# mLSTM heads' inverse root: one power operation on GpSimd in place of ScalarE's square root and VectorE's reciprocal

## What is computed

```python
h = num / jnp.maximum(jnp.abs(den), jnp.exp(-m_t))[..., None]
...
hm = mlstm_chunkwise(mq, mk, mv, log_i, log_f)
hm = rms_norm_2(hm, out_norm_g.reshape(M_HEADS, M_V_DIM)).reshape(B, L, M_WIDTH).astype(x.dtype)
ym = hm * jax.nn.sigmoid(mo) * jax.nn.silu(mgate)
...
y = jnp.concatenate([ya, ym], axis=-1) @ w_out.astype(x.dtype)
```

## Time and profile before

| | us |
|---|---|
| median of 3 runs | 1455.07 (1453.48 to 1455.53) |
| the profiled execution itself | 1452.7 |
| its span | 1450.9 |
| TensorE busy | 1431.7 (99%) |
| VectorE busy | 1092.5 (75%) |
| ScalarE busy | 853.9 (59%) |
| GpSimd busy | 273.1 (19%) |
| share of TensorE, VectorE, ScalarE in the chain that ended last | 88%, 7%, 3% |

### The profile page before, as it was taken

How to read it: one execution, slowest core, us unless ns; L and a number is a source line. 1 busy time by engine, 2 the same in 40 slices (tenths; PEclk the granted TensorE clock), 3 DMA queues, 4 the chain that set the end, 5 groups by cost and what they waited for, 6 DMA issues and landing times.

```text
span 1450.9 us, 27343 instructions
## 1 busy us (share of the span) xinstructions
PE 1431.7 (99%) x9657; PEld 1320.6 (91%) x9657; DVE 1092.5 (75%) x2021; ACT 853.9 (59%) x1559; POOL 273.1 (19%) x329
## 2 busy tenths in 40 slices
PE   8999999999999999999999999999999999999988
PEld 7888899988888888889988888999999999999988
DVE  6777679877766777667787766888778769876883
ACT  6665458766645656445566654556756555576752
POOL 1111113121111111024031112422240125121000
PEclk9999999999999999999999999999999999999999
DMA  6667754556655666555456656544344555434443
GB/s 212 200 189 211 239 178 132 182 178 200 191 188 181 193 190 187 186 192 174 147 177 199 197 165 181 169 132 115 98 128 136 168 146 147 140 90 136 133 129 119
DMA packets 247875, 241.25 MB, mean 166 GB/s; under 512 B 15456, under 2 KB 246736, under 8 KB 247784
## 3 DMA queue, kind: packets, MB, share of 16 engines
q1 hardware_dynamic: 244888, 236.73, 53.5%
q10 hardware_dynamic: 2896, 3.30, 0.8%
HBM read 238.92 MB, written 1.07 MB: 165 GB/s over the span
## 4 chain that ended last, share of the span: by engine, by line
PE 88%; DVE 7%; ACT 3%; issue 2%; DMA 1%; ACTq 0%; DVEq 0%
PE bank L652 79%; DVE w_lo L1818 2%; ACT w_hi L1084 1%; DVE work L2410 1%; PE bank L951 1%; PE bank L969 1%; PE bank L934 1%; PE bank L880 1%; DVE work L1851 1%; PE bank L890 1%; DVE work L2433 1%; ACT L1112 1%; PE bank L950 1%; DMA work<-in_x_dram 1%; PE bank L970 0%
## 5 line engine op out<-in xcount | busy, mean ns | idle before, releaser
L652 PE MATMUL bank<-x_both,w_hi 128*128 128x512 f32 (+2 forms) x3552 | 805.0, 332 | 0.5 <-DVE h L1914 0.5
L1818 DVE TENSOR_TENSOR w_lo<-raw,w_hi 128x1024 fp32r<-128x1024 f32 (+1 forms) x456 | 552.6, 1235 | 214.9 <-ACT w_hi L1084 213.9
L1084 ACT CAST w_hi<-raw 128x1024 fp32r<-128x1024 f32 (+1 forms) x456 | 457.1, 1029 | 135.7 <-PE bank L652 117.9
L652 PEld LDWEIGHTS bank<-x_both,w_hi 128*128 128x128 f32 x3552 | 515.1, 189 | 3.7 <-DVE w_lo L1818 0.6
L652 PE MATMUL bank<-x_both,w_lo 128*128 128x256 f32 (+1 forms) x2480 | 496.7, 281 | 0.0
L652 PEld LDWEIGHTS bank<-x_both,w_lo 128*128 128x128 f32 x2480 | 432.1, 189 | 62.6
L652 PE MATMUL bank<-y_both,w_hi 128*128 128x512 f32 (+2 forms) x1472 | 346.9, 338 | 5.7 <-DVE w_lo L1818 3.6
L652 PEld LDWEIGHTS bank<-y_both,w_lo 128*128 128x128 f32 x1088 | 191.7, 188 | 31.3
L652 PEld LDWEIGHTS bank<-y_both,w_hi 128*128 128x128 f32 x1472 | 213.3, 189 | 7.1 <-DVE w_lo L1818 4.5
L652 PE MATMUL bank<-y_both,w_lo 128*128 128x256 f32 (+1 forms) x1088 | 215.8, 280 | 0.0
L1705 POOL TENSOR_TENSOR work<-work,rstd 128x256 f32<-128x256 f32 x88 | 66.9, 781 | 412.3 <-ACT work L1149 412.3
(11 more groups left out here) (306 smaller groups left out, 1231.1 us busy)
## 6 DMA issues: line engine op xcount, KB each, us to landing
raw<-in_ffn_w_in_dram SPq DMA_DIRECT2D x176, 512.0 KB, 4.0
raw<-in_w_in_dram SPq DMA_DIRECT2D x100, 512.0 KB, 3.7
raw<-in_ffn_w_out_dram SPq DMA_DIRECT2D x64, 512.0 KB, 4.5
raw<-in_w_out_dram SPq DMA_DIRECT2D x32, 512.0 KB, 3.6
raw<-in_ffn_w_out_dram SPq DMA_DIRECT2D x32, 384.0 KB, 3.6
raw<-in_rec_w_in_dram SPq DMA_DIRECT2D x16, 512.0 KB, 4.2
raw<-in_sg_w_in_dram SPq DMA_DIRECT2D x16, 512.0 KB, 4.2
raw<-in_rec_w_out_dram SPq DMA_DIRECT2D x8, 512.0 KB, 3.5
```

What stands on the lines that cost most here:

```text
L652: i_ = mm(accs[m][:, cols], w[:, s, j, m * P:(m + 1) * P], moving, start=begin and g == 0 and not residual, stop=final)
L1084: nc.scalar.copy(w_hi[:, s, 0:n, :], raw[:, s, 0:n, :]).then_inc(hi_made, 1)
L1818: TT(w_lo[:, s, 0:n, :], raw[:, s, 0:n, :], w_hi[:, s, 0:n, :].bitcast(fp32), SUB).then_inc(lo_made, 1)
```

## The change

The inverse root becomes one operation on GpSimd, s_b = d_max ^ (-1/2), with the exponent from a one-column tile broadcast along the row. The factor 1/16 that ScalarE applied moves into the sum: TensorE's L1018 takes a broadcast column of 1/16 in place of ones, and VectorE's L2398 multiplies by 16 EPS in place of 256 EPS. ScalarE loses, per head, both table loads, both dummies and the root; VectorE loses the reciprocal. `taken` stays where it was and waits for GpSimd's `m_sb`. In `taken`'s place for heads 0 to 2 nothing else moves. ScalarE's square into d_max now waits for the previous head's power, since GpSimd reads that tile.

```diff
@@ TensorE, step 2
-                            i_ = mm(bank[5][:, 0:L], ones[:, :], n_sq[:, w, :], start=w == 0, stop=w == 1)
+                            i_ = mm(bank[5][:, 0:L], sixteenth[:, 0:1].broadcast_to((P, P)), n_sq[:, w, :], start=w == 0,
+                                    stop=w == 1)
@@ ScalarE, step 1, step 2 and head_root
                         i_.then_inc(m_sq, 1)
+                        if n:
+                            act.wait_ge(m_sb, n)
                         activation(d_max, bank[4][:, 0:L], ACT.Square).then_inc(m_dsq, 1)
                     if stage == 2:
-
-                        root_table()
                         roots_due.append(n)
...
-                        act.wait_ge(ms_read, n + 1)
                         if n % M_H < M_H - 1:
                             act.wait_ge(m_den, n + 1)
                             floor_to_all(l, n % M_H + 1)
-                        if n:
-                            act.wait_ge(m_sb, n)
-                        activation(d_root, d_max, ACT.Sqrt, scale=1.0 / 16).then_inc(m_root, 1)
-                        exp_table()
@@ GpSimd, start
             nc.gpsimd.memset(eps_sq[:, :], EPS * EPS)
+            nc.gpsimd.memset(sixteenth[:, :], 1.0 / 16)
+            nc.gpsimd.memset(minus_half[:, :], -0.5)
             nc.gpsimd.memset(epsc[:, :], EPS).then_inc(ones_set, 1)
@@ GpSimd, end of each layer
                     pool.wait_ge(h_final, NC8)
+                for n in range(M_H * l, M_H * (l + 1)):
+                    pool.wait_ge(ms_read, n + 1)
+                    if n:
+                        pool.wait_ge(m_taken, n)
+                    TT(s_b, d_max, minus_half[:, 0:1].broadcast_to((P, L)), POW).then_inc(m_sb, 1)
+                if l == 0:
                     h_squares(7, "proj0", 0)
@@ VectorE, step 2, inverse_root, taken
-                        STT(out=d_max, in0=d_max, scalar=256 * EPS, in1=bank[5][:, 0:L], op0=MUL, op1=ADD).then_inc(ms_read, 1)
+                        STT(out=d_max, in0=d_max, scalar=16 * EPS, in1=bank[5][:, 0:L], op0=MUL, op1=ADD).then_inc(ms_read, 1)
...
-                def inverse_root(n):
-
-                    dve.wait_ge(m_root, n + 1)
-                    V.reciprocal(s_b, d_root).then_inc(m_sb, 1)
-
                 def taken(hd, stage):
                     n = M_H * l + hd
                     if stage == 3:
-                        if hd == M_H - 1:
-                            inverse_root(n)
                         dve.wait_ge(m_sb, n + 1)
...
                                 if n[0]:
-                                    inverse_root(M_H * l + n[0] - 1)
                                     taken(n[0] - 1, 3)
```

More of the change, by code:

```diff
@@ L230, in build_stack @@
     ALU, ACT = mybir.AluOpType, mybir.ActivationFunctionType
-    MUL, ADD, SUB, MAX, MIN = ALU.mult, ALU.add, ALU.subtract, ALU.max, ALU.min
+    MUL, ADD, SUB, MAX, MIN, POW = ALU.mult, ALU.add, ALU.subtract, ALU.max, ALU.min, ALU.pow
     dram = dict(ffn1_w_in=ffn1_w_in, ffn1_w_out=ffn1_w_out, ffn2_w_in=ffn2_w_in, ffn2_w_out=ffn2_w_out,
@@ L270, in build_stack @@
         x_sums = sb("x_sums", [P, 2])
+        sixteenth = sb("sixteenth", [P, 1])
+        minus_half = sb("minus_half", [P, 1])
         work = sb("work", [P, WORK_SLOTS * L])
```

## The result

| | before | after |
|---|---|---|
| median of 4 runs each, same chip | 1454.28 us (1453.37 to 1455.53) | 1766.49 us (1765.70 to 1768.44) |
| ratio, 95% interval | | 1.2151 (1.2136 to 1.2166) |
| span of the profiled execution | 1450.9 us | 1763.9 us |

The kernel became 312.2 us slower, where 7.2 us of gain were forecast and the range ended at 1487. The page of the changed kernel first: busy times, granted clock, shares of the chain that ended last, and the groups of the power and of `taken` (busy, mean ns | idle before and its releaser). The edit moved the lines: L2398 of before is L2404, L2372 is L2378, L2386 is L2392, L2421 is L2420, L2433 is L2432, L1009 is L1011, L1018 is L1020, L652 is L654, L1818 is L1824; L2441 is L2440, L2446 is L2445, L2456 is L2455; the power is L1801.

What follows compares the result with a forecast made beforehand. VectorE's loop, slower than TensorE's by 0.85 and 1.34 us a head, was taken to bound the head stretches. TensorE's 7.7 us of idle less 0.5 gave -7.2 us, from 1455.07 to 1447.9 us; range 1446 to 1451, 8 in 10 to 1487.

Steps and rivals of the forecast that it cites:

- The price of the power: GpSimd's power over 128x272, once per head: 2.8 us, as 4.3 times a product's 0.64 us.
- The forecast's upper end: Far end taken for GpSimd's power: twenty product passes, 12.8 us, giving a kernel time of about 1520 us.
- the slow rival: VectorE stands at `taken` between heads, TensorE behind it; 6 us per us of power beyond 3.7; chance 0.40.
- the prediction's free formula: Without contention: six times r's excess over 3.87 us between heads, twice `taken`'s lateness against 9.31 us behind last heads.
- r = power + 0.2: Time from the sum step's end (L2398) to `taken`: the power plus two handovers of 0.1 us, 3.0 us.
- The forecast's own case: A power of 2.8 us closes nearly all TensorE waits in the heads' stretches: -7.2 us, 1447.9 us.
- the 7.7 us of idle: TensorE's idle in the two mLSTM head stretches, claimed as all the change can give back.
- the 0.5 us off for contention: Taken off the gain for what may be left of layer 1's 3.3 us of projection waits.
- The cover of the squares: Squares queued on GpSimd behind the fourth power, released 21 us after L2398; a longer power would bare them.
- Contention: Behind last heads, GpSimd's power may lock out VectorE's two-input steps throughout, `taken` coming 4.5 + power after L2398; even chance.

Runs made afterwards that it cites:

- 40 columns: The changed kernel with the power over 40 of the 272 columns, the other 232 left out: 1468.37 us, ratio 1.0099.
- the run with the product: The changed kernel with the power turned into a GpSimd product of the same shape, the inverse root left out: 1442.76 us, ratio 0.9924.
- 17 columns: The changed kernel with the power over 17 of the 272 columns, the other 255 left out: 1442.61 us, ratio 0.9925.
- the run of shapes: The kernel before with five extra GpSimd powers of different shapes on their own tiles, nobody waiting for them: 1453.45 us, ratio 1.0005.

## Why the prediction was wrong

- **The step that failed is "The price of the power".** It took 4.3 times a product, 2.8 us, from the ratio of VectorE's reciprocal to VectorE's maximum. The measured price is 43.75 us, 68 products and 16 times the step's value. The forecast's upper end, twenty products or 12.8 us, was chosen and not read from a row; the truth lies 3.4 times beyond it, and so the range of the time failed too. The neighbouring row came from another engine, on which the reciprocal is one instruction of 1.85 us; GpSimd's rows had only sums, products and memsets and said nothing of a function. The prediction said that itself ("nothing in the trace bounds a function made of many steps") and then bounded it.
- **The mechanism was right**, that of the slow rival: VectorE standing at `taken`, w_lo and the next scores queued behind it, TensorE waiting for these. With the measured 43.8 us the prediction's free formula gives 6 x (43.81 - 3.87) = 239.6 between heads and 2 x (43.94 - 9.31) = 69.3 behind the last, 308.9 us together; measured 312.2. For 40 columns it gives +13.3 against +14.7. What it left out is the slower clock after the stalls, which can explain a rest of this size (3.6 us behind the last heads).
- **The small terms.** The prediction took r = power + 0.2; it is power + 0.11. The sum step's new constant and the broadcast column of L1020 cost nothing that was seen, as costed; the run with the product has both and is fast.
- **The forecast's own case** (a power near 2.8 us) was run with 17 columns: it gains 11.1 us, where 7.2 were forecast for it. Here the 7.7 us of idle, by the prediction "all that a change here can give back", was too small: TensorE's weight loads waited 10.2 us. And the 0.5 us off for contention wasn't due.
- **The cover of the squares** held at 43.8 us, though the prediction had it bared from 21: the power and the squares' own release moved together, since the projection waits for the same power. The squares start at 1302.57, 12 us after the power's end.
- **Contention**: the prediction took from the earlier trace rows that each engine keeps the other out for the whole instruction. Beside a power only the step at its start is longer: L2432 1.23 us in place of 0.79 and L2378 1.03 in place of 0.56 with 272 columns, 0.84 and 0.64 with 40. Why it goes with the columns is open. The next w_lo, 1.8 us into the power of 43.8 us, takes its usual 1.22. The Trainium skill (SBUF - State Buffer, SBUF: two separate sides) has the shared pair of ports held for the whole instruction by whichever starts first, a GpSimd instruction that reads SBUF or a VectorE one with two SBUF inputs. For the power the traces differ from it (1.22 us for a w_lo in the middle of 43.8 us), and the measurement decides.

## What to carry to other kernels

An operation on an engine that has never run it in your traces has no price: a ratio from another engine isn't one. Run it by itself, at two sizes, before a dependency hangs on it; off the path it disturbs nothing, as the run of shapes shows. Look first for a function of the engine that already does the neighbouring step (ScalarE's reciprocal square root at 0.41 us in place of 0.41 + 1.85 on two engines), and for what merely stands behind the slow step in a queue: moving w_hi ahead of the root was worth 5.4 us with no new operation. Read the possible gain from the waits of the weight loads as well as from those of the matmuls: here they showed 10.2 us and 7.8, and 11.0 were to be had. And before you add an engine's slower work to a loss, look who waited for it.

## What the runs showed of the hardware

- GpSimd's power in fp32 takes 0.34 us + 0.1594 us a column, whatever the number of partitions (8 or 128) and whatever the exponent (-0.5 or 2.0). The Trainium skill (GPSIMD Engine Reference, Performance versus the Vector engine) gives a core 16 lanes, reckons with 1.2 GHz and puts a branch that depends on data at about 12 cycles an element. By that, an estimate, 16 elements one after the other would be 192 cycles, and the measured 0.1594 us is 191. That they are worked through one by one, and all 16 even when only 8 partitions are asked for, no run here shows. Since the cost is by the column and d_max holds the same values on every partition, a layout with the tokens over the partitions would need three columns. It wasn't tried.
- A long GpSimd instruction doesn't have to hold VectorE back: 81 us of powers beside it left the kernel's time at a ratio of 1.0005 (0.9996 to 1.0014), and only the VectorE step at a power's start took longer, by 0.3 to 0.5 us with 272 columns. The product of the earlier trace rows did lengthen the w_lo beside it, from 1.23 to 1.63 us.
- TensorE came out of each stall of 34 to 39 us with its matmuls at 1.2 GHz: 1.8 us more busy time after each at a projection and 2.7 us after each between heads. With 40 columns the same was seen behind waits of 3.56 and 4.06 us, with the granted clock at 0.50 over the twelve matmuls (3.81 us), and not behind those of 1.97 and 2.28 us (2.03 us).
